# The dilated stage of a two-block kernel: a key's attention in slots behind the next key's products, separate PSUM banks for both, and the combining of pieces shared by two engines

## The reference, cut to what matters

```python
proj = rms_norm(x, norm_w) @ w_in            # u_f, g_f, q, k, v, g_a
q = rms_norm(q per head, q_norm_w) / 8;  k = rms_norm(k per head, k_norm_w)
for c, (window, dilation) in enumerate(((128, 1), (512, 4), (2048, 16))):
    # 8 heads of 64 each; query t sees keys t + j*dilation, |j| <= 64, with a linear bias
    outs[c], lses[c] = dilated_window_attention(q[c], k[c], v[c], window, dilation, slopes)
alpha = softmax(stack(lses), axis=0)         # over the three configurations
o = sum(alpha * outs);  y_a = o * silu(g_a)
```

## Time and profile before

| what | value |
|---|---|
| median of 3 runs (lowest to highest) | 3410.51 us (3409.1 to 3413.03) |
| span of the profiled execution | 3412.3 us |
| PE busy | 3307.3 us, 97% of the span |
| PE weight loads | 1809.4 us, 53% |
| DVE, ACT, POOL busy | 1310.2, 1015.7, 928.4 us (38, 30, 27%) |
| dilated stage, first product to last attention | some 1611 to 2957 us |
| granted TensorE clock in the stage | 1.00 |

### The profile page before, as it was taken

One profiled execution on the slowest core, in us unless ns is written; L12 is line 12 of the kernel. 1 busy time (PEld: TensorE's weight loads), 2 busy tenths in 40 slices (PEclk: granted clock), 3 DMA queues, 4 the chain that ended last, 5 costly groups with the idle time before them and its releaser, 6 DMA issues. The chain is left out here.

```text
span 3412.3 us, 43811 instructions
## 1 busy us (share of the span) xinstructions
PE 3307.3 (97%) x16379; PEld 1809.4 (53%) x16379; DVE 1310.2 (38%) x2804; ACT 1015.7 (30%) x2409; POOL 928.4 (27%) x705
## 2 busy tenths in 40 slices
PE   8999999998999999898999999999999999999999
PEld 4485858584455455444454545454545454545544
DVE  3334444446244244444333323332433243545522
ACT  4314141413324144233233423342334143411100
POOL 1002020205442532633311152115211521161232
PEclk9999999999999999999999999999999999999999
DMA  6101010113021112332061646254634464340321
GB/s 226 35 25 38 21 38 13 33 41 96 25 48 20 49 31 83 122 108 79 22 35 32 40 100 51 32 45 106 43 29 49 108 40 26 59 117 13 142 93 62
DMA packets 282365, 202.43 MB, mean 59 GB/s; under 512 B 124380, under 2 KB 249708, under 8 KB 278528
## 3 DMA queue, kind: packets, MB, share of 16 engines
q1 hardware_dynamic: 279052, 199.62, 30.8%
q10 hardware_dynamic: 3104, 0.01, 0.1%
HBM read 153.79 MB, written 45.81 MB: 58 GB/s over the span
## 5 line engine op out<-in xcount | busy, mean ns | idle before, releaser
L2465 PE MATMUL d<-hT,roll 128*128 128x512 f32 x1280 | 579.4, 596 | 2.1 <-PEq L76 2.1
L2465 PE MATMUL d<-w_room,roll 128*128 128x512 f32 x960 | 435.6, 596 | 2.3 <-DVE w_room L2429 2.3
L2465 PEld LDWEIGHTS d<-hT,roll 128*128 128x128 f32 x1280 | 242.4, 191 | 300.8 <-issue 299.3
L600 PE MATMUL m<-hT,roll 128*128 128x512 f32 x704 | 321.1, 593 | 1.3 <-ACT pre L750 1.3
L2465 PEld LDWEIGHTS d<-w_room,roll 128*128 128x128 f32 x960 | 181.1, 190 | 224.6 <-issue 222.8
L2502 POOL TENSOR_TENSOR w_z<-w_u,w_y 128x512 f32<-128x512 f32 x40 | 50.7, 1267 | 796.4 <-ACT w_y L2471 787.3
L1412 PE MATMUL n<-hT,roll 128*128 128x512 f32 x512 | 227.6, 600 | 1.8 <-PEq L76 1.8
L600 PEld LDWEIGHTS m<-hT,roll 128*128 128x128 f32 x704 | 124.9, 191 | 116.0 <-issue 115.8
L1412 PE MATMUL n<-mix_na,roll 128*128 128x512 f32 x384 | 169.4, 594 | 0.5 <-POOL roll L1312 0.5
L548 POOL TENSOR_TENSOR hn<-hn 128x512 f32<-128x512 f32 x16 | 17.5, 1093 | 543.3 <-DVE hn L917 543.3
L1412 PEld LDWEIGHTS n<-hT,roll 128*128 128x128 f32 x512 | 97.1, 192 | 123.3 <-issue 122.9
(11 more groups left out here) (403 smaller groups left out, 5205.8 us busy)
## 6 DMA issues: line engine op xcount, KB each, us to landing
roll<-in_w_in SPq DMA_DIRECT2D x128, 256.0 KB, 3.1
mix_f<-alpha SPq DMA_DIRECT2D x48, 192.0 KB, 6.1
xg<-in_x SPq DMA_DIRECT2D x4, 2048.0 KB, 16.2
roll<-in_w_in SPq DMA_DIRECT2D x16, 512.0 KB, 3.8
rb<-r_rows SPq DMA_DIRECT2D x16, 512.0 KB, 4.8
mix_ml<-in_x SPq DMA_DIRECT2D x16, 512.0 KB, 3.3
x<-mix_ml SPq DMA_DIRECT2D x16, 512.0 KB, 3.0
o_rows<-mix_f SPq DMA_DIRECT2D x8, 1024.0 KB
```

The source lines that it names most:

```text
L600: last = nc.tensor.matmul(bank[n % 2][:], w[:, k], hT[:, k, (n % 4) * TB:(n % 4 + 1) * TB], start=(k == 0), stop=(k == KC - 1))
L2465: last = nc.tensor.matmul(bank[self.bank_of(n, j, i)][:], w[:, k], x[k], start=(k == 0), stop=(k == h - 1))
```

## The change

- A projection's products use banks 2 and 3 alone, scores banks 0 and 1. Product i waits for the product two before it. Scores k wait for all minima of group k-1.
- Attention a-1 is cut into slots 1 to 11. On PE slot s comes behind product s of the keys projection of a (7 products of half 0, then half 1). Slot 1: `turn_values` 0, 1; slot 2: `turn_values` 2, 3; slot k+2: `turns(k)`, `scores(k+2)`, `values(k-1)`. Scores 0 and 1 come behind products 6 and 7 of the second half of the projection before. The sums are at products 5 and 7 of half 0 and 1, 2, 4, 6, 7 of half 1.
- POOL combines pieces 0, 2, 4 and DVE pieces 1, 3, 5, 7, 6 of pairs 0 to 2, with semaphores of their own. DVE does so between the additions of the values projection. The factors are made at the end of the first keys projection instead of in its first half, and before `make_first`.
- SP's order is changed to fit: `load(n+3, 0)` and `load(n+5, 0)` now follow the statistics' stores, and pieces are fetched and kept in the order 1, 0, 3, 2, 5, 4, 7, 6.

```diff
-    BANKS = 4
+    FIRST_BANK, BANKS = 2, 2
...
-        if i == 1:
-            need(pe, self.held, 2 * s)
-        elif i == 5:
-            pe.wait_ge(self.held, 2 * s + 1)
+        if i in (3, 6):
+            pe.wait_ge(self.held, 2 * s + {3: 1, 6: 2}[i])
         else:
-            need(pe, self.full, 5 * s + {2: -2, 3: -1, 4: 0, 6: 1, 7: 2}[i])
+            need(pe, self.full, 5 * s + {1: -1, 2: 0, 4: 1, 5: 2, 7: 3}[i])
...
+    def taker(self, g, m):
+        if g == PAIRS - 1:
+            return 0, 3 * g + m
+        return (1, 5 * g + {1: 0, 3: 1, 5: 2, 7: 3, 6: 4}[m]) if m in (1, 3, 5, 6, 7) else (0, 3 * g + m // 2)
```

SP, for a pair g > 0 (`keep_piece` and `fetch_piece` wait for the piece that they follow):

```diff
+                        load(n + 1, 0)
                         store_turned_stats(g - 1)
                         late.fetch_stats(sp, t, g - 1)
...
                         late.fetch_rows(sp, t, g - 1, 0)
                         late.fetch_rows(sp, t, g - 1, 1)
+                        load(n + 1, 2)
+                        fetch_bias(g)
+                        load(n + 1, 3)
                         late.store_alpha(sp, t, g - 1)
                         late.fetch_alpha(sp, t, g - 1, 0)
                         late.fetch_alpha(sp, t, g - 1, 1)
+                        late.fetch_piece(sp, t, g - 1, 3)
                         late.fetch_piece(sp, t, g - 1, 2)
+                        late.keep_piece(sp, t, g - 1, 1)
                         late.keep_piece(sp, t, g - 1, 0)
+                        late.fetch_piece(sp, t, g - 1, 5)
+                        late.keep_piece(sp, t, g - 1, 3)
+                        store_y(n + 1, 0, v_dst)
+                        store_z(n + 1, 0, v_dst)
                         late.fetch_piece(sp, t, g - 1, 4)
                         late.keep_piece(sp, t, g - 1, 2)
                         late.fetch_piece(sp, t, g - 1, 7)
                         late.keep_piece(sp, t, g - 1, 5)
                         load(n + 2, 1)
                         load(n + 2, 0)
+                        late.fetch_piece(sp, t, g - 1, 6)
...
                     load(n + 3, 1)
                     store_stats(a)
+                    load(n + 3, 0)
                     store_rows(a)
-                    load(n + 3, 0, 2, 3)
+                    load(n + 3, 2, 3)
...
                     load(n + 5, 1)
                     store_stats(a + 1)
+                    load(n + 5, 0)
                     store_rows(a + 1)
...
-                    load(n + 5, 0, 2, 3)
+                    load(n + 5, 2, 3)
```

POOL, DVE and PE:

```diff
+                    if n > 0:
+                        join(n, 0, 1)
+                    if mixing:
+                        late.combine(pool, nc.gpsimd, g - 1, 2)
+                    if n > 0:
+                        join(n, 0, 2)
+                    if mixing:
+                        late.mixed_by(pool, g - 1, 7)
+                        nc.gpsimd.memset(prob, 0.0).then_inc(zeroed, 1)
+                        late.combine(pool, nc.gpsimd, g - 1, 4)
+                    join(n, 1, 1)
+                    join(n, 1, 2)
+                    if weighing:
+                        late.factors_pool(nc, pool, g - 1)
                     seven.make_first(nc, pool, n + 1)
+                    if weighing:
+                        late.weights_pool(nc, pool, g - 1)
                     seven.make_last(nc, pool, n + 1)
+                    if weighing:
+                        pool.wait_ge(out, NB * N_CFG * g)
+                        late.combine(pool, nc.gpsimd, g - 1, 0)
...
                 def project_values(a):
...
                     for j in range(2):
...
                         add(n, j, 2)
                         if j == 0:
                             need(dve, pv, NB * a)
+                            need(dve, out, NB * a)
+                            combine(1)
+                        else:
+                            combine(6)
                         add(n, j, 3, cols(0))
+                        if j == 0:
+                            combine(3)
                         add(n, j, 5)
                         add(n, j, 6)
+                        if j == 0:
+                            combine(5)
+                        else:
+                            start(a, 0)
                         add(n, j, 7, cols(1))
+                        if j == 0:
+                            combine(7)
+                        else:
+                            start(a, 1)
...
+                    if slot == 1:
+                        if cfg(a) == 0:
+                            sums(a, 7)
+                        turn_values(a, 0)
+                        turn_values(a, 1)
+                    elif slot == 2:
+                        turn_values(a, 2)
+                        turn_values(a, 3)
+                    k = slot - 2
+                    if 0 <= k < NB:
+                        turns(a, k)
+                    if 0 <= k < NB - 2:
+                        scores(a, k + 2)
+                    if 0 < k <= NB:
+                        values(a, k - 1)
```

More of the change, by code:

```diff
@@ L3075, in _ @@
                         project_values(a)
-                    attend(a)
-                for step in range(3):
-                    tail(NA - 1, step)
+                for slot in range(1, NB + 3):
+                    attend(NA - 1, slot)
             @block.scalar
@@ new lines, in project_keys @@
+                    for slot in (1, 2, 3):
+                        attend(a - 1, slot)
+                    hold(n, 0, 4)
+                    square(a, 0)
+                    for slot in (4, 5):
+                        attend(a - 1, slot)
+                    root(a, 0)
+                    square(a, 1)
+                    for slot in (6, 7):
+                        attend(a - 1, slot)
+                    root(a, 1)
+                    square(a, 2)
+                    hold(n, 1, 1)
+                    attend(a - 1, 8)
@@ new lines, in project_keys @@
+                    root(a, 2)
+                    square(a, 3)
+                    attend(a - 1, 9)
+                    root(a, 3)
+                    square(a, 4)
+                    hold(n, 1, 4)
+                    root(a, 4)
+                    square(a, 5)
+                    root(a, 5)
+                    square(a, 6)
+                    root(a, 6)
+                    if g > 0 and a % N_CFG == 0:
+                        late.factors_act(nc, act, g - 1)
+                    if cfg(a) == 0:
+                        square(a, 7)
+                        for k in range(2):
+                            for i in range(BU):
+                                exps(a, k, i)
@@ L3206, in _ @@
                         project_values(a)
-                    attend(a)
-                copies(NA - 1, NB - 2)
-                keep_stats(PAIRS - 1)
-                copies(NA - 1, NB - 1)
+                for slot in range(1, NB + 2):
+                    attend(NA - 1, slot)
             @block.vector
@@ L3266, in write_out, with start, attend @@
                     nc.vector.tensor_copy(dst, src).then_inc(out, 1)
-                def tail(a, step):
+                def start(a, k):
+                    if k == 0:
+                        if a % N_CFG == 0:
+                            dve.wait_ge(bias_in, 48 * (a // N_CFG + 1))
+                        if a >= N_CFG:
+                            dve.wait_ge(late.st_stored, 16 * stat_stores(a))
+                    for i in range(BU):
+                        biased_min(a, k, i)
+                def attend(a, slot):
@@ L3269, in tail @@
                     if a < 0:
                         return
-                    if step < 2:
-                        copies(a, NB - 2 + step)
-                    write_out(a, NB - 3 + step)
+                    if slot == 1 and cfg(a) == 0:
+                        norm(a, 7)
+                    if slot == 2:
+                        for m in range(2, 4):
+                            dve.wait_ge(v_turned, 4 * a + m + 1)
+                            if a % N_CFG == 0 and m == 2:
+                                late.pair_mixed(dve, a // N_CFG)
+                            nc.vector.tensor_copy(vals[:, 4 * m:4 * m + 4], bank[T_BANK + m][:, :].rearrange("p (c l) -> p c l", l=P)).then_inc(v_dve, 1)
@@ new lines, in project_keys, with project_values, combine @@
+                    add(n, 1, 7)
+                    norm(a, 6)
+                    if weighing:
+                        late.invert_dve(nc, dve, g - 1)
+                    if cfg(a) == 0:
+                        start(a, 0)
+                        start(a, 1)
+                def project_values(a):
+                    n, g = keys_of(a) + 1, a // N_CFG
+                    mixing = g > 0 and a % N_CFG == 0
+                    def combine(m):
+                        if mixing:
+                            late.combine(dve, nc.vector, g - 1, m)
@@ L3344, in _ @@
                         project_values(a)
[L3345 to L3348 removed]
+                for slot in range(1, NB + 4):
```

(1 more changed line is left out.)

347 lines of the change are left out of this document (130 added, 217 removed).

## The result

The changed kernel takes 3585.38 us (median of 4 runs, 3575.62 to 3593.68) against 3411.6 for the kernel before on the same chip: ratio 1.0505, with a 95% interval of 1.0493 to 1.0517. It is slower by 174 us, 42 above the forecast of 3543 and inside the range 3445 to 3615. The profiled execution is the fastest of the four, 9.8 us under their median, so the trace has 161.5 of the 174 us to explain; the rest is the spread from one execution to the next.

The account below looks back on a forecast made before the run. TensorE, busy 97% of the span, bounds the kernel, with only 31 us of pauses to win. Slots -23, scores(1) +13, queue +20 and +36, combining +86 sum to +132: 3543 us, range 3445 to 3615.

Parts of the forecast that it names:

- The direction: Whole kernel: the change makes it slower, chance 0.86 together; faster 0.10, same 0.04.
- Combining: Value projections of three pairs: products wait for additions queued behind VectorE's pieces awaiting loads; 28.8 us each, +86 us.
- Scores(1): End of dilation-1 keys: scores(1) wait for VectorE's minima after norm 6; 3.2 us, 4 times, +13 us.
- The slots: Attention behind keys' products: 31 us of TensorE pauses go, 8 us of switches come; net -23 us.
- The queue: Statistics' stores delay loads behind them: +20 at the gates' first tiles, +36 at values and tiles of next keys.
- the priced 45 for these seven places: Part of the queue's price: 5 us at four gates' projections, 8.3 us at three pairs' next keys.
- if the vector engines keep pace: Condition on the slots' 31 us gain; VectorE and ScalarE work was judged to fit, some 4.5 in 6.2 us.
- The signs: Expected trace: late products 5 and 7, alpha waits some 5 us, waits for minima, tiles, v_rows; clock 1.00.
- The port (case 4): VectorE and GpSimd combining side by side exclude each other: +2.1 us for 15 pieces, +31, 3574 us; chance 0.14.

Follow-up runs that it names:

- Run 4: Changed kernel with even pieces on GpSimd, odd on VectorE, each placed where its loads have landed, make_first ahead of the factors: 3485.54 us (1.0218).
- run 8: Kernel before the change with the combining of pairs 0 to 2 left out: 3411.97 us (0.9996).
- run 1: Changed kernel with the combining of pairs 0 to 2 left out, dilation 1's output stored instead: 3448.84 us (1.0108).
- Run 12: Run 9's kernel with dilation 16's statistics stores in two halves, the first earlier: 3407.31 us (0.9984).
- run 9: Changed kernel without combining of pairs 0 to 2, write-outs at their own slot's end, dilation 1's scores(1) one product later: 3464.6 us (1.0149).
- Run 5: Changed kernel with write-outs in their own slot, dilation 1's scores(1) one product later, and pieces placed where loads have landed: 3467.95 us (1.0161).
- run 2: Changed kernel with each write-out at the end of its own slot instead of behind the next slot's addition: 3543.33 us (1.0394).
- run 11: Run 5's kernel with combining factors some 14 us earlier, and dilation 16's statistics stores in two halves, the first earlier: 3414.53 us (1.0008).
- run 7: Run 5's kernel with combining factors some 14 us earlier, and the next first-tile loads queued ahead of the statistics' stores: 3492.1 us (1.0238).
- run 10: Run 5's kernel with factors some 14 us earlier, first-tile load between stores of maxima and sums, piece 5 one addition later: 3493.22 us (1.0238).

## Why the prediction was right, and where it was not

**The direction and the largest term: right.** Combining was +86: 28.8 us in each of three pairs, from a landing of 7.6 us and the order of additions. Measured: 30.4, 31.9 and 30.7, 93 in all, with VectorE's waits of 7.69 to 9.28 us for four of the first pair's five pieces. The first piece began 19.5 us after the keys' last product, as predicted. By product the prediction said 1.2, 5.8, 3.2, 3, 3, 12.6; the trace has 1.90, 7.20, 0.73, 4.55, 3.45, 12.55. Run 4 shows that the landing in VectorE's order is the cause, run 8 that it was new.

**Scores(1), +13: right**, 3.36 us a time in run 1. In the changed kernel the line is 20: the first of the four stood 0.9 longer behind a norm of 1.67 us instead of 0.75, and 5.1 are the stores' landing.

**The slots, -23: right in the end, but not at once.** In the changed kernel the balance leaves -15 for them, at the upper bound (161.7 less 93 for combining, 30 for write-outs, 20 for scores(1), 3 for tiles and 31 for the half clock). Run 12 against run 8 has them nearly alone: 4.7 us of net gain, on top of 5.7 of `make_first`, 3.4 of the last scores(1), 7.4 of tiles and 5.1 of half clock, which are other terms. So the slots are worth some 26 us (22 by the two traces; an estimate). Alternating costs matmuls of 512 columns 9.4 us there, where 8 were predicted. Two banks are enough: products of run 12 wait 0.6 us for additions.

**The queue, +56: the step that failed is its place in a sum.** The queue's times were right: in the changed kernel the first tile landed 34.5 to 41.2 us after the first store, 36.5 estimated. And without pauses the gates' first product is due 33 us after it (run 9; 32 predicted). But in the changed kernel that product came 35 us after it, since the slots had waits for write-outs, and the pairs' first product had the pause of scores(1) ahead of it. These pauses gave the tiles their time, and TensorE stood only 8 us for the queue: 3 for tiles and values, 5 inside scores(1). The sum added the pause of scores(1) and the queue as if both would be waited for. Take the pauses away and the queue costs 48 us (run 9), near the priced 45 for these seven places. The pairs' first product is then due at 32 us and not at the predicted 36, and tiles land after 36 to 48 us; why some land later than in the changed kernel is open. So the terms were not additive. Run 5 shows the same thing from the other side.

**Missing, +30 and +31.** That `values(k-1)` waits for `write_out(k-2)`, which VectorE reaches only behind the next slot's addition, can be read in the code; "if the vector engines keep pace" passed over it. It cost 30 us (run 2). The half clock behind pauses, +31, could have been read in the trace of before as the price of the few pauses that it has (4.7 us), but was not carried over. The forecast's sum mends to 132 - 48 (queue) + 30 + 31 + 7 (combining) + 2 (scores) + 8 (slots) = 162. These are 30 of the 42 us by which the median lies above the forecast; the other 12 are the spread of the executions. Errors of both signs, -48 and +78, met on the way: that the range held was in part luck.

**The signs.** The products named stood, and VectorE waited for alpha, 7.7 us and more where 5 were said. But TensorE waited only 2.4 us for tiles and 0.5 for `v_rows`, and the clock of the stage was 0.96 and not 1.00.

**The port (case 4)** was given 0.14 and +31. VectorE's piece at 2037.97 ran beside GpSimd's piece (2035.99 to 2040.96): its five instructions ended 4.7 us after its start, where those of the one at 2050.95, alone, took 2.4. So the trace agrees that the engines delay each other, 0.83 to 1.37 us for an instruction of 0.42. The Trainium skill (SBUF — State Buffer, "Who interferes with whom") says that such instructions exclude each other for their whole length. The record doesn't show it so strictly: 0.42 and 0.72, one after the other, would be 1.14 us, and VectorE's third to fifth instruction start 0.86 apart. And only the first piece of a pair met GpSimd so (4.68, 4.77 and 4.27 us), about 2.2 us three times, and not fifteen times 2.1 as the case had it.

## What to carry to other kernels

An instruction that waits for a transfer must not stand in an engine's order ahead of work that another engine waits for: placed where the transfer had landed, the same work cost 100 us less (run 4), and with the other waits mended and the stores spread 171 (run 11). Terms that share a deadline are not added: when a pause goes, ask which transfer loses its cover, as run 9 shows, where curing two waits of 44 us made the kernel slower. And where all is just in time, a load moved ahead of stores can cost more than it brings (runs 7 and 10); spreading the stores cured it (run 11).

## What was not expected of the hardware

- **Long pauses cost more than their length.** The changed kernel's stage has 16 pauses of 3.2 to 12.6 us, 103 us in all, and at 15 of them the granted clock was 0.5 for 3.4 to 13.7 us around their end; a product took 6.54 us after one instead of 3.6. Over the stage that was 31 us. Taking away the short waits for write-outs (at most 1.5 us each) changed it by 1.5 us (run 2).
- **Stores of single elements, in eight DMAs of 1024.** Issued at once, the last four held SP for 12.0 us (changed kernel) to 18.5 us (run 9), and the load behind them landed 34.5 to 47.6 us after the first. In two sets of half the size, 22 us apart, none was held (2.6 to 3.2 us for four).
